# Moving the scatter of an expert pair between the two contraction halves of the next pair's gate and up products

## The chip, the cores and the metric

The kernel runs on one core of a Trainium2 chip. The metric is the device time of one execution in microseconds; the median of three runs stands for the kernel. It is written against the engines directly: each engine has its own program, and they meet only at semaphores.

## The reference, cut to what matters

The kernel computes one inference step of a two-layer backbone over 128 context and 128 latent tokens with 1024 channels. Each layer has two token mixers (attention and gated linear attention) and then a mixture of experts with 16 experts of width 512, of which two are chosen for each token inside its best group. All is float32. The change touches only the mixture of experts:

```
gates = jnp.sum(jax.nn.one_hot(top_idx, N_EXPERTS, dtype=jnp.float32) * top_w[..., None], axis=1)
act = jax.nn.silu(jnp.einsum('nd,edf->nef', hf, w_gate)) * jnp.einsum('nd,edf->nef', hf, w_up)
y = jnp.einsum('nef,efd->nd', act * gates[..., None].astype(act.dtype), w_down)
x = x + g2 * y
```

## The kernel before, in words

The dense part of a layer comes first, then the experts, in pairs: 8 pairs a layer, each with two experts of 64 token slots (with these inputs one pass is enough, since the trace shows 16 pairs in both layers). `expert_pair` on TensorE (L1000 to L1069) does for a pair q:

- the gate and up products (L1023) of the gathered rows `hg`, over 1024 channels in two contraction halves, kh 0 and kh 1, each in two parts and for two halves of the expert's columns. Half 0 of the columns is complete three quarters of the way through kh 1, half 1 at its end;
- `turn(0)` (L1044): the transposes of the activated half 0 of the columns, `aa`, into a PSUM bank. It waits for VectorE's activation (`m_act`) of that half;
- `scatter(q - 1)` (L971 to L983, products at L981), not in the first pair: the previous pair's output rows `yy`, 64 slots of each expert, times the turned gates `gwt`, which spreads them to their tokens. Eight products into the PSUM banks 4, 5, 7 and again 4; the last group waits until VectorE has added the first (`m_x`);
- `turn(1)` for half 1 of the columns;
- the down products (L1035) in two halves. Each waits for ScalarE's copy of its turned columns (`m_at_copied`) and for its weights. The first pair has `sort_rows` (L996) between them;
- `turn_gates(q)` (L968), the transposes of the gates that the next scatter needs.

After the last pair of a pass `scatter` is called once more, by itself (L1078).

ScalarE (`expert_pair`, L1342 to L1370) does for a pair, in this order: two sigmoids of the gate columns (L1347); the copy of turn 0 (recorded at the helper line L1092); then, behind it in its program, the `windows` for the next pair, for which it loads six registers from `starts` (L1306) and makes four copies of sorted rows into `hg`; the copy of turn 1; two copies of the down products into `yy`; the copy of the turned gates.

```
for half in range(2):
    act.wait_ge(m_at[l], q * 2 + 2 + half)
...
    copy(at_[:, 2 * half:2 * half + 2, :],
...
    elif half == 0:
        windows(q + 1, window_starts(pr + 1))
```

VectorE does `activate(q)` (L1856 and L1858, for each half of the columns one product with the gate and one with the up columns), `add_experts(q - 1)` (L1867: 16 instructions that add the scattered rows, scaled, to x) and `onehots` (L1843) for the next pair.

SyncE (SP) loads the weights. The pairs have 6 units of 2 MiB: units 0 and 1 are the gate and up weights of kh 0 for the two experts, 2 and 3 those of kh 1, 4 and 5 the two halves of the down weights. Each is loaded in two parts of 1 MiB (L441) into a ring of six slots, so a part can be loaded only when the previous pair has used that part of its unit; `expert_use` gives the semaphore for it. SP waits for one part after the other, in the order in which PE uses them. Units 0, 1 and 2 of pair 4 have a place of their own (`MORE`) and are loaded ahead of pair 0's products. Behind the last pair the next layer's dense units use the same ring.

Of the kernel before, what the change touches and what calls it, by code (L numbers as in the profile page):

```python
# [212 lines left out]
def build(nc, xT, consts, params, lparams, w_ada, w_in, w_pa, w_pb, w_out, w_gu, w_down,  # L213
# [4 lines left out]
    with ctx:  # L218
# [189 lines left out]
        def gu_unit(l, kh, e, in_more):  # L408
            return expert_space(l, 2 * kh + e, in_more).rearrange("p (c j k n) -> p c j k n", c=2, j=2, k=KH // 2)

        def down_unit(l, half):
            return expert_space(l, 4 + half, False).rearrange("p (e k n) -> p e k n", e=2, k=FT // 2)
# [114 lines left out]
        def _(pe):  # L527
# [120 lines left out]
            for l in range(LAYERS):  # L648
# [313 lines left out]
                def turn_gates(q):  # L962

                    pe.wait_ge(m_onehot[l], q + 2)
                    pe.wait_ge(m_x[l], q * 4 + X_DONE)
                    pe.wait_ge(m_gwt_copied[l], q + 1)
                    for s in range(S):
                        mm = pe.transpose(ps[:, 7, s * P:(s + 1) * P], gw[:, s, :], ident)  # L968
                    mm.then_inc(m_gwt[l], 1)

                def scatter(q):  # L971

                    pe.wait_ge(m_gwt_copied[l], q + 2)
                    for f in range(4):
                        if f % 2 == 0:
                            pe.wait_ge(m_y[l], q * 2 + 2 + f // 2)
                        if f in (0, 3):
                            pe.wait_ge(m_x[l], q * 4 + (1 if f else 0) + X_DONE)
                        for j in range(2):
                            k = 2 * f + j  # L980
                            mm = pe.matmul(ps[:, (4, 5, 7, 4)[f], j * NT:(j + 1) * NT], yy[:, k * P:(k + 1) * P], gwt,  # L981
                                           start=True, stop=True)
                        mm.then_inc(m_scat[l], 1)  # L983
# [16 lines left out]
                def expert_pair(pss, pr, in_more=False, later=False, first=False):  # L1000
                    q = pss * PAIRS + pr

                    pe.wait_ge(m_act[l], q * 2 + 1)
                    for kh in range(2):
                        for e in range(2):
                            u = 2 * kh + e
                            if u not in MORE:
                                pe.wait_ge(moe_full[l][u], q * 32 + 32)
                            elif in_more:
                                pe.wait_ge(more_full[l][u], pss * 32 + 32)  # L1010
                            else:

                                loads = pr if later else pr + 1
                                pe.wait_ge(moe_full[l][u], pss * (32 * (PAIRS - 1)) + loads * 32)
                        if kh == 0:
                            pe.wait_ge(m_hg[l], q * 4 + 5)
                        for part in range(2):
                            for half in range(2):
                                for kk in range(KH // 2):
                                    k = kh * KH + part * (KH // 2) + kk  # L1020
                                    for e in range(2):
                                        r = e * SLOTS
                                        mm = pe.matmul(ps[r:r + SLOTS, half, :].rearrange("p (j n) -> p j n", j=2),  # L1023
                                                       hg[:, k, e, 0:SLOTS],
                                                       gu_unit(l, kh, e, in_more)[:, part, :, kk, half * 256:(half + 1) * 256],
                                                       start=k == 0, stop=k == KT - 1)
                                if kh and part:
                                    mm.then_inc(m_gu[l][half], 1)
                            if not (kh and part):
                                mm.then_inc(m_rows[l], 1)  # L1030

                    def down(k, n):
                        for e in range(2):
                            r = e * SLOTS
                            mm = pe.matmul(ps[r:r + SLOTS, 2 + n, :], at_[:, k, r:r + SLOTS],  # L1035
                                           down_unit(l, k // 2)[:, e, k % 2, n * 512:(n + 1) * 512],
                                           start=k == 0, stop=k == FT - 1)
                        return mm

                    def turn(half):  # L1040
                        pe.wait_ge(m_act[l], q * 2 + 2 + half)
                        pe.wait_ge(m_at_copied[l], q * 2 + 1 + half)
                        for j in range(2):
                            mm = pe.transpose(ps[:, 6, (2 * half + j) * P:(2 * half + j + 1) * P],  # L1044
                                              aa[:, half, j * P:(j + 1) * P], ident)
                        mm.then_inc(m_at[l], 1)

                    turn(0)
                    if not first:
                        scatter(q - 1)  # L1050
                    turn(1)
                    pe.wait_ge(m_y[l], q * 2 + 1)
                    for half in range(2):
                        pe.wait_ge(m_at_copied[l], q * 2 + 2 + half)
                        pe.wait_ge(moe_full[l][4 + half], q * 32 + 32)
                        if half == 0:
                            for k in range(2):
                                for n in range(2):
                                    mm = down(k, n)
                            mm.then_inc(m_dn[l][0], 1)  # L1060
                            if first:
                                sort_rows(pss)
                        else:
                            for n in range(2):
                                down(2, n)
                                down(3, n).then_inc((m_dy[l], m_dn[l][1])[n], 1)
                    if first:
                        pe.wait_ge(m_rowcopied[l], pss * (2 * ROWS // P) + 2 * ROWS // P)
                    turn_gates(q)  # L1069
# [310 lines left out]
        def _(dve):  # L1380
# [132 lines left out]
            for l in range(LAYERS):  # L1513
# [336 lines left out]
                def activate(q):  # L1850

                    for half in range(2):
                        dve.wait_ge(m_sig[l], q * 2 + 2 + half)
                        dve.wait_ge(m_at[l], q * 2 + 1)
                        gate, up, e = ps[:, half, 0:256], ps[:, half, 256:512], eg[:, half, :]
                        dve.tensor_tensor(e, e, gate, ALU.mult).then_inc(m_silu[l], 1)  # L1856
                        dve.wait_ge(m_silu[l], q * 2 + 1 + half)
                        dve.tensor_tensor(aa[:, half, :], e, up, ALU.mult).then_inc(m_act[l], 1)  # L1858

                def add_experts(q):  # L1860

                    for f in range(4):
                        dve.wait_ge(m_scat[l], q * 4 + f + 2)
                        for j in range(2):
                            for s in range(S):
                                k, c = 2 * f + j, slice(s * T, (s + 1) * T)
                                ins = dve.scalar_tensor_tensor(  # L1867
                                    x[:, k, c], ps[:, (4, 5, 7, 4)[f], j * NT + s * T:j * NT + (s + 1) * T],
                                    mod[:, l, 40 + k, s:s + 1], x[:, k, c], ALU.mult, ALU.add)
                        ins.then_inc(m_x[l], 1)  # L1870
# [21 lines left out]
                with dve.Fori(0, passes) as pss:  # L1892
                    first = pss * PAIRS
                    activate(first)
                    onehots(1, first + 1)
                    with dve.Fori(1, PAIRS - 1) as pr:
                        q = pss * PAIRS + pr
                        activate(q)
                        add_experts(q - 1)
                        onehots(pr + 1, q + 1)  # L1900
                    last = pss * PAIRS + (PAIRS - 1)
                    next_windows(pss)
                    activate(last)
                    add_experts(last - 1)
                    onehots(0, last + 1)
                    add_experts(last)
                dve.wait_ge(m_x[l], passes * (4 * PAIRS) + X_DONE)
# [200 lines left out]
```

## Time and profile before

| | us |
|---|---|
| median of 3 runs (lowest, highest) | 1016.75 (1015.66, 1017.27) |
| the profiled execution: its time | 1016.9 |
| the profiled execution: its span | 1015.1 |
| PE busy in the span | 965.7 |
| VectorE busy | 383.4 |
| ScalarE busy | 237.9 |
| share of the hardware DMA queue in 16 engines' span | 75.1% |

All rows come from the one profiled execution, and times in them are counted from the start of its span; what lies around the span is 1.8 us. The experts of layer 0 stand at about 296 to 518 us, those of layer 1 at about 789 to 1012 us. PE is the product engine, PEld its weight loads, DVE is VectorE, ACT is ScalarE, SP is SyncE. A wait is named with its releaser: what ended it. "Issue" is time in which an engine waited for nothing that the profile shows. L1092 is the line of a helper that makes all of ScalarE's copies; its tiles tell which copy it is (`tmq` holds `hg`, `yy`, `at_` and `gwt`; a copy from `cst` is a window copy).

### The profile page before, as it was taken

How to read it: one execution, taken by the hardware profiler on the slowest of the kernel's cores; microseconds unless marked ns; L12 is line 12 of the kernel's file. 1: busy time of each engine (PE TensorE's matmuls, PEld its weight loads, DVE VectorE, ACT ScalarE, POOL GpSimd, SP SyncE). 2: the span in 40 equal slices, each digit the busy share in tenths (PEclk: the TensorE clock that was granted, in tenths of full speed). 3: DMA queues.
4: the chain of work that ended last, by engine and by line, in shares of the span. 5: the costliest groups of instructions: out<-in, count | busy, mean ns of one | idle time of the engine just before them, and what ended most of it. 6: DMA issues, size and time to landing. Idle time of an engine off the chain costs nothing.

```text
span 1015.1 us, 13671 instructions
## 1 busy us (share of the span) xinstructions
PE 965.7 (95%) x4910; PEld 566.2 (56%) x4910; DVE 383.4 (38%) x1011; ACT 237.9 (23%) x521; POOL 99.9 (10%) x85
## 2 busy tenths in 40 slices
PE   9999999989989999999899999999899899999997
PEld 3458876767845443443344688777686444344333
DVE  4098513782261222222351421248635222222134
ACT  2213223520023222221140312343201222222121
POOL 0000004631100000000000000066310000000000
PEclk9999999999999999999999999999999999999999
DMA  9999462156999999999997524240877999989993
GB/s 391 383 397 410 181 247 97 72 235 243 403 367 407 410 422 363 424 421 423 426 425 323 223 94 157 83 167 1 343 287 285 401 402 423 423 363 422 421 422 124
DMA packets 37378, 317.48 MB, mean 313 GB/s; under 512 B 4280, under 2 KB 4432, under 8 KB 5328
## 3 DMA queue, kind: packets, MB, share of 16 engines
q1 hardware_dynamic: 36144, 311.28, 75.1%
q0 software_dynamic: 1184, 5.53, 1.3%
q8 instruction: 32, 0.52, 0.2%
q14 instruction: 18, 0.15, 0.0%
HBM read 314.93 MB, written 1.86 MB: 312 GB/s over the span
## 4 chain that ended last, share of the span: by engine, by line
PE 77%; DMA 13%; DVE 4%; ACT 3%; issue 1%; SPq 0%; ACTq 0%; DVEq 0%
PE ps L1023 18%; DMA ring<-w_gu 12%; PE ps L563 11%; PE ps L1035 7%; PE ps L717 7%; PE ps L912 5%; PE ps L981 3%; PE ps L898 3%; PE ps L735 3%; PE ps L830 2%; PE ps L576 2%; PE ps L996 1%; DMA ring<-w_ada 1%; PE ps L673 1%; PE ps L543 1%
## 5 line engine op out<-in xcount | busy, mean ns | idle before, releaser
L1023 PE MATMUL ps<-ring,tmq 128*64 128x512 f32 x928 | 214.1, 602 | 17.2 <-DMA ring<-w_gu 13.7
L1023 PEld LDWEIGHTS ps<-ring,tmq 128*64 128x64 f32 x928 | 68.2, 138 | 143.6 <-issue 126.1
L563 PE MATMUL ps<-more,ring 128*128 128x256 f32 x512 | 114.3, 381 | 0.5 <-ACT more L1092 0.5
L1035 PE MATMUL ps<-ring,tmq 128*64 128x512 f32 x512 | 113.8, 596 | 0.0
L563 PEld LDWEIGHTS ps<-more,ring 128*128 128x128 f32 x512 | 96.1, 190 | 15.5 <-issue 2.5
L1856 DVE TENSOR_TENSOR tmq<-tmq,ps 128x256 f32<-128x256 f32 x32 | 13.5, 422 | 206.5 <-ACT tmq L1347 206.5
L1092 ACT ACTIVATE tmq<-ps 128x256 f32<-128x256 f32 (+3 forms) x124 | 55.6, 462 | 149.0 <-PE ps L717 62.8
L1035 PEld LDWEIGHTS ps<-ring,tmq 128*64 128x64 f32 x512 | 35.2, 137 | 65.7 <-issue 62.1
L717 PE MATMUL ps<-ring,more 128*128 128x512 f32 (+1 forms) x192 | 69.9, 523 | 0.0
L1867 DVE SCALAR_TENSOR_TENSOR x<-ps,mod,x 128x128 f32<-128x128 f32 x256 | 67.6, 342 | 1.9 <-PE ps L981 1.9
L1347 ACT ACTIVATE tmq<-ps 128x256 f32<-128x256 f32 x32 | 12.3, 384 | 226.6 <-PE ps L1023 226.6
L1843 DVE TENSOR_SCALAR tmq<-cst,st 128x64 f32<-128x64 f32 x72 | 17.8, 310 | 117.9 <-PE ps L968 117.2
L981 PE MATMUL ps<-tmq 128*128 128x256 f32 x256 | 58.6, 382 | 1.6 <-ACT tmq L1092 1.6
L912 PE MATMUL ps<-more,ring 128*128 128x256 f32 x256 | 56.4, 380 | 0.0
L717 PEld LDWEIGHTS ps<-ring,more 128*128 128x128 f32 x192 | 36.2, 190 | 32.9 <-issue 31.1
L912 PEld LDWEIGHTS ps<-more,ring 128*128 128x128 f32 x256 | 48.2, 190 | 7.1 <-issue 0.8
L981 PEld LDWEIGHTS ps<-tmq 128*128 128x128 f32 x256 | 47.3, 190 | 8.0 <-issue 2.0
L1092 ACT ACTIVATE tmq<-cst 128x512 f32 (+1 forms) x64 | 35.3, 622 | 47.9 <-issue 47.6
L1942 POOL TENSOR_TENSOR more<-tmq,cst 128x896 f32<-128x896 f32 x16 | 33.3, 2084 | 119.1 <-PE ps L766 109.4
L1479 DVE SCALAR_TENSOR_TENSOR wide<-ring,mixer 128x1024 f32<-128x1024 f32 x32 | 39.2, 1224 | 10.6 <-DMA mixer<-cs_dram 9.6
L543 PE MATMUL ps<-ring,cs 128*32 128x512 f32 x320 | 39.7, 611 | 1.0 <-DMA ring<-w_ada 1.0
L1956 POOL TENSOR_TENSOR mixer<-tmq,more 128x896 f32<-128x896 f32 x16 | 35.2, 2200 | 49.5 <-ACT more L1240 31.2
(256 smaller groups left out, 1036.0 us busy)
## 6 DMA issues: line engine op xcount, KB each, us to landing
ring<-w_gu SPq DMA_DIRECT2D x116, 1024.0 KB, 14.3
ring<-w_down SPq DMA_DIRECT2D x64, 1024.0 KB, 12.4
ring<-w_ada SPq DMA_DIRECT2D x24, 2048.0 KB, 10.9
ring<-w_in SPq DMA_DIRECT2D x14, 2048.0 KB, 17.1
ring<-w_out SPq DMA_DIRECT2D x4, 2048.0 KB, 11.1
more<-w_gu SPq DMA_DIRECT2D x8, 1024.0 KB, 14.1
cst<-consts SPq DMA_DIRECT2D x2, 2080.0 KB, 15.8
ring<-w_in SPq DMA_DIRECT2D x4, 1024.0 KB, 24.1
```

The source lines that it names most:

```text
L543: mm = pe.matmul(ps[j:j + 32, 7, :], cs[:, k, :], w[:, k, :], start=k < 4, stop=k >= 4)
L563: mm = pe.matmul(ps[:, 5, i * NT:(i + 1) * NT], w[:, k, m * P:(m + 1) * P], h[:, k, :], start=k == 0, stop=k == KT - 1)
L717: mm = pe.matmul(ps[:, n % 4, 0:cols], h[:, k, (n % 2) * T:(n % 2) * T + T], w[:, k, 0:cols], start=i == 0, stop=i == KT - 1)
L912: mm = pe.matmul(ps[:, 4 + b % 4, (b // 4) * NT:(b // 4 + 1) * NT], w[:, k, (b % 4) * P:(b % 4 + 1) * P], sga[:, k, :], start=k == 0, stop ...
L981: mm = pe.matmul(ps[:, (4, 5, 7, 4)[f], j * NT:(j + 1) * NT], yy[:, k * P:(k + 1) * P], gwt, start=True, stop=True)
L1023: mm = pe.matmul(ps[r:r + SLOTS, half, :].rearrange("p (j n) -> p j n", j=2), hg[:, k, e, 0:SLOTS], gu_unit(l, kh, e, in_more)[:, part, :, ...
L1035: mm = pe.matmul(ps[r:r + SLOTS, 2 + n, :], at_[:, k, r:r + SLOTS], down_unit(l, k // 2)[:, e, k % 2, n * 512:(n + 1) * 512], start=k == 0 ...
L1092: return act.activation(out, in_, ACT.Copy, scale=scale)
L1479: link(dve.scalar_tensor_tensor(wide[:, :], w[:, i, :], 1.0, cs_rows[:, s, :], ALU.mult, ALU.mult, accum_out=mod[:, l, 4 * a + i, s:s + 1]))
L1867: ins = dve.scalar_tensor_tensor(x[:, k, c], ps[:, (4, 5, 7, 4)[f], j * NT + s * T:j * NT + (s + 1) * T], mod[:, l, 40 + k, s:s + 1], x[:, ...
L1942: pool.tensor_tensor(qz, q, C("side").rearrange("p (v t) -> p v t", t=T), ALU.mult).then_inc(g_qz, 1)
L1956: pool.tensor_tensor(halves(ke), kh.unsqueeze(1).to_broadcast([P, LEVELS, 2, HALF]), level_view(e), ALU.mult).then_inc(g_ke, 1)
```

## The change

In TensorE's program the scatter of the previous pair is called between kh 0 and kh 1 of the gate and up products, no longer between the two turns. In VectorE's program the adds of the previous pair, which read what the scatter wrote, come ahead of the activation, in the loop and for the last pair. The first pair of a pass, ScalarE's program and SP's program are as before.

```
--- before.py
+++ after.py
@@ -1028,6 +1028,8 @@
                                     mm.then_inc(m_gu[l][half], 1)
                             if not (kh and part):
                                 mm.then_inc(m_rows[l], 1)
+                        if kh == 0 and not first:
+                            scatter(q - 1)
 
                     def down(k, n):
                         for e in range(2):
@@ -1046,8 +1048,6 @@
                         mm.then_inc(m_at[l], 1)
 
                     turn(0)
-                    if not first:
-                        scatter(q - 1)
                     turn(1)
                     pe.wait_ge(m_y[l], q * 2 + 1)
                     for half in range(2):
@@ -1895,13 +1895,13 @@
                     onehots(1, first + 1)
                     with dve.Fori(1, PAIRS - 1) as pr:
                         q = pss * PAIRS + pr
+                        add_experts(q - 1)
                         activate(q)
-                        add_experts(q - 1)
                         onehots(pr + 1, q + 1)
                     last = pss * PAIRS + (PAIRS - 1)
                     next_windows(pss)
+                    add_experts(last - 1)
                     activate(last)
-                    add_experts(last - 1)
                     onehots(0, last + 1)
                     add_experts(last)
                 dve.wait_ge(m_x[l], passes * (4 * PAIRS) + X_DONE)
```

## Rows read from the trace of the kernel before

**Rows 1.** The page, busy time of an engine and the DMA share by slices
```profile
PE 965.7 (95%) x4910; PEld 566.2 (56%) x4910; DVE 383.4 (38%) x1011; ACT 237.9 (23%) x521; POOL 99.9 (10%) x85
...
DMA  9999462156999999999997524240877999989993
```

**Rows 2.** The chain that ended last, shares of the span by engine
```profile
PE 77%; DMA 13%; DVE 4%; ACT 3%; issue 1%; SPq 0%; ACTq 0%; DVEq 0%
```

**Rows 3.** The list of waits: who waited for whom, total us, times, longest
```profile
PE ps L1023 <- DMA ring<-w_gu: 13.7, 7, 2.7
```

**Rows 4.** Windows: stretch, its us, busy PE, PEld, DVE, ACT, POOL, clock, DMA, GB/s
```profile
326.38:351.74 25.36, 25.36 (x120) 10.39 (x119) 6.87 (x24) 5.11 (x12) 0.00 (x0) 1.00 0.98 398
...
377.08:404.06 26.98, 25.57 (x119) 10.26 (x118) 6.87 (x24) 5.10 (x12) 0.00 (x0) 1.00 0.91 368
...
404.00:454.00 50.00, 50.00 (x236) 20.57 (x234) 13.72 (x48) 9.99 (x22) 0.00 (x0) 1.00 1.01 422
...
326.38:513.70 187.32, 179.86 (x827) 72.80 (x826) 49.46 (x176) 35.64 (x78) 0.00 (x0) 0.99 1.00 412
819.42:1005.44 186.02, 179.80 (x827) 72.67 (x826) 49.36 (x176) 35.63 (x78) 0.00 (x0) 0.99 0.94 387
```

**Rows 5.** Timeline of PE, pairs 6 and 7: start, us, work, idle time before it
```profile
463.70 7.09 PE L1023 MATMUL ps<-ring,tmq 128*64 128x512 f32 x32 [1.86 <-DMA ring<-w_gu]
...
483.76 7.09 PE L1023 MATMUL ps<-ring,tmq 128*64 128x512 f32 x32 [1.51 <-DMA ring<-w_gu]
...
493.53 8.78 PE L1023 MATMUL ps<-ring,tmq 128*64 128x512 f32 x32 [2.68 <-DMA ring<-w_gu]
```

**Rows 6.** Timeline of pair 1 around its turns
```profile
340.27 0.44 PE L1044 MATMUL ps<-cst,tmq 128*128 128x128 f32 x2
...
340.54 3.66 PE L981 MATMUL ps<-tmq 128*128 128x256 f32 x16
...
340.82 0.38 ACT L1092 ACTIVATE tmq<-ps 128x256 f32<-128x256 f32 x1
...
341.65 4.23 DVE L1867 SCALAR_TENSOR_TENSOR x<-ps,mod,x 128x128 f32<-128x128 f32 x16
344.04 0.38 PE L1044 MATMUL ps<-cst,tmq 128*128 128x128 f32 x2
344.35 7.09 PE L1035 MATMUL ps<-ring,tmq 128*64 128x512 f32 x32
344.67 2.22 ACT L1092 ACTIVATE tmq<-cst 128x512 f32 x4 [3.46 <-issue]
346.79 0.36 ACT L1092 ACTIVATE tmq<-ps 128x256 f32<-128x256 f32 x1
```

**Rows 7.** One line, L1306: count, duration in ns min/median/max, first and last start
```profile
L1306 ACTq TENSOR_LOAD <-starts x96: 271/278/297, 310.4 to 997.3; - x96
```

**Rows 8.** Timeline of pair 0, which has no scatter, around its turns
```profile
309.68 0.44 PE L1044 MATMUL ps<-cst,tmq 128*128 128x128 f32 x2
...
311.13 0.44 PE L1044 MATMUL ps<-cst,tmq 128*128 128x128 f32 x2 [1.02 <-DVE tmq L1858]
...
311.50 3.65 PE L1035 MATMUL ps<-ring,tmq 128*64 128x512 f32 x16
```

**Rows 9.** The chain in order of time at the kernel's end: start, us, what
```profile
1005.68 0.39 ACT tmq L1092
1006.06 0.23 issue
1006.29 1.14 PE ps L981 x4
```

**Rows 10.** The line of the weight loads, L441: from issue to landing
```profile
DMA to landing us min/median/max: 4.9/14.1/22.7
```

**Rows 11.** Windows after waits of PE in layer 1, columns as in group 4
```profile
985.00:990.00 5.00, 3.05 (x14) 1.06 (x16) 0.00 (x0) 0.00 (x0) 0.00 (x0) 1.00 1.01 421
...
957.20:966.00 8.80, 8.80 (x33) 2.68 (x34) 0.84 (x2) 0.40 (x2) 0.00 (x0) 0.81 1.02 425
```

More of the change, by code:

```diff
@@ L1030, in expert_pair @@
                                 mm.then_inc(m_rows[l], 1)
+                        if kh == 0 and not first:
+                            scatter(q - 1)
                     def down(k, n):
@@ L1048, in expert_pair @@
                     turn(0)
-                    if not first:
-                        scatter(q - 1)
                     turn(1)
@@ L1897, in _ @@
                         q = pss * PAIRS + pr
+                        add_experts(q - 1)
                         activate(q)
-                        add_experts(q - 1)
                         onehots(pr + 1, q + 1)
@@ L1902, in _ @@
                     next_windows(pss)
+                    add_experts(last - 1)
                     activate(last)
-                    add_experts(last - 1)
                     onehots(0, last + 1)
```

## The prediction

> **What bounds the kernel now.** I read the page first. TensorE (PE) is busy 95% of the span, and the DMA row of the slices stands at 9, once at 8, in both expert stretches (about the 12th to 20th and the 32nd to 39th slice) [rows 1]. So the product engine and the weight stream both run nearly full there, and the change touches only those stretches. The chain that ended last is PE for 77% and DMA for 13% [rows 2], and the list of waits gives the DMA part a place: the gate and up products waited for w_gu units, 7 times, 13.7 us in all [rows 3]. The windows by expert pair then say which of the two leads when. A pair that waits for nothing takes PE 25.36 us [rows 4]. A pair needs 12 parts of 1 MiB; at the 422 GB/s of the undisturbed stretch that is 2.48 us a part, 29.8 us a pair [rows 4]. So PE is the quicker by 4.4 us, starts with a stock of loaded units, and eats it up: the waits of the timeline come in pairs 6 and 7 (1.86, 1.51 and 2.68 us) [rows 5], and in pair 3 the same. From the start of pair 1's products to the end of pair 7 a layer takes 187.32 and 186.02 us, where seven pairs without a wait would take 177.5 [rows 4]. So 9.8 and 8.5 us a layer are waits for weights, with some slower products after them.
>
> The last view is the timeline around the two turns (the transposes of the activated halves) in pair 1: what stands in the place from which the scatter is taken. Turn 0 starts at 340.27 (I call this moment t), the scatter runs 340.54 to 344.04, turn 1 follows, and the down products start at 344.35, t + 4.08 [rows 6]. Under that scatter ScalarE (ACT) and VectorE (DVE) finish the second half's activation, and ACT then does more: the copy of turn 0 at 340.82, a gap of 3.46 us put down to "issue", four window copies (2.22 us), and only then the copy of turn 1, at 346.79 to 347.15, t + 6.88 [rows 6]. The gap is no idle time: it holds the six register loads of the window starts (96 TENSOR_LOADs in 16 pairs) and the arithmetic on them [rows 7]. The second half of the down products waits for that last copy. Today it comes at t + 4.08 + 3.51 = t + 7.59, half of the 7.09 us row and then some, so the copy is ready about 0.7 us early [rows 6]. **That small margin exists only because of the scatter.**
>
> **The change, part by part.** The scatter itself is moved, not changed: 8 products, 16 PE instructions, 3.50 us from its first product to turn 1 [rows 6]. It issues no DMA; its waits (the turned gates, the two halves of the y rows) are signalled while kh 0's first products still run. PE pays 3.50 us there and is spared 3.50 here, net 0. Borders of its new place aren't in the trace: I bound them by -0.1 us (the weights of neighbours overlap as well as here) and +0.3 us a pair (turn 1 costs 0.31 us with its borders, 344.04 to 344.35 [rows 6]); I take 0, since the scatter's own rows show no gap at either border.
>
> Turn 1 without cover. The trace of before already has one pair in the new order: pair 0, which has no scatter. There turn 0 starts at 309.68, turn 1 at 311.13 after a wait of 1.02 us for DVE, the down products at 311.50, which is t + 1.82 [rows 8]. The scatter's removal gives back 4.08 - 1.82 = 2.26 us, not 3.50. Cost: 3.50 - 2.26 = +1.24 us a pair.
>
> The copy of turn 1. Nothing on ACT moves: its order is still copy, loads, windows, copy, counted from turn 0, so it ends at t + 6.88 as now. The first half of the down products now ends at t + 1.82 + 3.51 = t + 5.33. A product waiting for ACT starts 0.23 us after the copy's end, by the one hand-over that the chain shows [rows 9]. So the second half starts at t + 7.11, a **new wait of 1.78 us** a pair (1.5 if the hand-over is free). Behind it stand, on PE, the second down half, the gate turns and the next pair's products, so nothing covers it.
>
> DVE. The adds of the previous pair (4.23 us [rows 6]) move ahead of the activation. They start about 1 us into the scatter and end some 2 us after it, while the first half's gate and up products need 5.2 us after the scatter, half of kh 1 and half of the rest (5.2 = three quarters of 7.0). So the activation isn't delayed; the cover is those products. Cost 0. The scatter's last product group waits for the first adds, which come as early as before. Cost 0.
>
> The sum on PE. A pair takes 25.36 + 1.24 + 1.78 = 28.38 us. Seven pairs take 198.7 us from the same starts: layer 0 ends its pairs at 326.38 + 198.7 = 525.1 instead of 513.70, +11.4; layer 1 at 819.42 + 198.7 = 1018.1 instead of 1005.44, +12.7. Pair 0 is as before, and so is everything after the pairs.
>
> Do waits for weights still add to that? SP is moved past nothing, but its buffers come free later: the kh 1 units by 3.50 us, the last down unit 0.8 us earlier in the pair. What matters is whether the stream, now slower than PE by only 1.5 us a pair, still runs PE down. The stream ran dry once a layer, before pair 4, whose first three units were loaded ahead (368 GB/s in that pair) [rows 4]. By my times it is dry last when pair 3's first down half is done: pair 3 starts at 383.1, its turn 0 comes 13.89 + 3.50 = 17.4 us later, and its first down half ends 5.33 us after that, at 405.8. The fastest landing took 4.9 us against 2.48 of transfer [rows 10], so the stream restarts at about 408 and then moves 40 parts without a break (4 for pair 4, 12 each for pairs 5 to 7). Those that close a need are the 20th, the 32nd and the 36th: pair 6's first units have landed by 408 + 20 x 2.48 + 2 = 460 against a need at 468.3; pair 7's at 489 against 496.7; pair 7's kh 1 units at 499 against 507.1. So PE is never starved; it has 7 us to spare at the tightest place, and the expert stretch turns from stream-bound to PE-bound. The stream ends about 6 us later than now, PE about 11, so the next layer's first units are no closer to being late.
>
> Total: 11.4 + 12.7 = 24.1 us; the profiled execution took 1016.9 us (span 1015.1), 0.15 above the median of 1016.75, so **1016.9 + 24.1 = 1041.0 us**. Own range of this case: 14 pairs by -0.35 us (border -0.1, hand-over free) to +0.3 us give 1036 to 1045.
>
> **The rivals.** 1. *The clock.* The new order puts two waits, 1.02 and 1.78 us, into 7 us of each pair. After the waits of 1.51 and 2.68 us in pair 7 its kh 1 products took 8.78 instead of 7.0 us [rows 5], and the stretch 957.2 to 966 after a wait had a granted clock of 0.81 [rows 11], a mix of the 1.2 and 2.4 GHz levels. If each pair fell so once, 14 x 1.78 = 25 us more, 1066; if half of them did, 1053. Against it: 985 to 990 has PE idle for 1.95 us and kept 1.00 [rows 11], and pair 6 waited 1.86 us before kh 1 and still took 7.0 us for it (463.70 to 470.7) [rows 5], so a wait as long as the longer new one needn't cost it. Chance 0.12. The Trainium skill (TensorE: Matmul & The Clock Gate, section HAM oscillation — how this bites in real kernels) describes loops in which waits between groups of products throttle the array anew in every iteration. [...]
>
> 2. *The margin isn't lost.* If the copy of turn 1 came earlier (its loads running ahead of turn 0), the second wait is gone and a pair takes 26.6 us. Seven take 186.2: 512.6 and 1005.6, so layer 0 gains 1.1 and layer 1 nothing. If turn 1 too were covered the stream would be the bound and the scatter would have left the tail behind the last landing: 493.53 + 7.0 + 1.82 + 7.02 + 0.35 = 509.7, 4.0 us early, and 2.3 in layer 1. So 1010.6 to 1015.5, **faster or the same**; it decides at a pair of 26.6 us, the least that the stream and the ends of before leave room for. Against it: the loads start only after the copy of turn 0 at every turn of rows 6 and 7, and ACT's program has them behind it. Chance 0.08, of it 0.05 faster by over 0.2%.
>
> 3. *In part.* The loads take less time where they don't run beside the scatter, and the wait is 0.5 to 1.2 us: 18 to 8 us less than the forecast, 1023 to 1033. Chance 0.06.
>
> **How the numbers follow.** The forecast has 0.74, and its time is the predicted one. The range takes its own range, the milder half of rival 1 and the upper part of rival 3: 1030 to 1053; left out are rival 2, the worst of rival 1 and half of rival 3. A measurement of this kernel can tell about 0.2% (2 us) from no change. Faster 0.05; same 0.03; slower 0.74 + 0.12 + 0.06 = 0.92.
>
> **What would show it.** Right: pair windows of 28.4 us at clock 1.00; PE L1023 no longer waiting for DMA; a new wait of PE L1035 for ACT's copy, 1.8 us in 14 pairs, and of turn 1 for DVE, 1.0 us; the slices' DMA rate lower in the expert stretches. The second half starting before t + 6.9, or pairs of 26.5 us, would make rival 2 right; a granted clock below 0.95 over the expert pairs, rival 1; waits for w_gu that stay would mean that I have the stream's slack wrong.

## The result and the profile after

The changed kernel takes 1043.76 us (median of 4 runs, 1042.61 to 1047.02), the kernel before 1017.01 us beside it: a ratio of 1.0248, with a 95% interval of 1.0218 to 1.0278. It is slower by 2.5%. The forecast was 1041.0 us in a range of 1030 to 1053. The profiled execution took 1043.26 us (span 1041.4), 26.4 us more than that of before.

The page of the changed kernel, first its busy times, DMA slices and chain, then two of the costliest groups:

```profile
PE 971.4 (93%) x4910; PEld 562.7 (54%) x4910; DVE 383.7 (37%) x1011; ACT 237.8 (23%) x521; POOL 99.9 (10%) x85
...
DMA  9999454076999997999995442242687999799991
...
PE 81%; ACT 5%; DVE 4%; ACTq 4%; issue 4%; DMA 1%; SPq 0%; DVEq 0%
...
L1023 PE MATMUL ps<-ring,tmq 128*64 128x512 f32 x928 | 212.2, 595 | 3.5 <-issue 3.5
L1037 PE MATMUL ps<-ring,tmq 128*64 128x512 f32 x512 | 116.9, 598 | 19.1 <-ACT tmq L1092 19.1
```

PE's busy time has hardly grown (971.4 against 965.7 us); the rest is idle. The DMA part of the chain has gone from 13% to 1%, and ACT with its queue, 3% before, is at 9% [rows 2]. The gate and up products wait for no weights any more [rows 3]; in their place the down products (L1037 is L1035 of before) wait 19.1 us for a copy of ScalarE. The list of waits of the changed kernel puts that beside the second new wait (us in total, times, longest):

```profile
PE ps L1037 <- ACT tmq L1092: 19.1, 14, 1.4
PE ps L1046 <- DVE tmq L1858: 16.4, 16, 1.0
```

The first has 14 instances, one in each pair that has a scatter. The second is turn 1 waiting for VectorE's activation: 16 times now, where only the two first pairs had it before.

The windows of single pairs and of both layers' seven pairs (columns as in group 4 of the rows):

```profile
325.66:354.23 28.57, 26.10 (x120) 10.11 (x119) 6.89 (x24) 5.10 (x12) 0.00 (x0) 1.00 0.99 400
...
382.77:411.32 28.55, 26.10 (x119) 10.10 (x119) 6.90 (x24) 5.10 (x12) 0.00 (x0) 1.00 0.73 277
325.66:525.07 199.41, 182.70 (x827) 70.73 (x826) 49.67 (x176) 35.66 (x78) 0.00 (x0) 1.00 0.97 398
832.33:1031.78 199.45, 182.69 (x827) 70.72 (x826) 49.55 (x176) 35.61 (x78) 0.00 (x0) 1.00 0.88 361
```

Pair 1 takes 28.57 us where it took 25.36 [rows 4], and every later pair takes the same: the seven last 199.41 us, 7 x 28.5. In pair 3 the weight stream now runs at 277 GB/s (368 before) and PE still waits for no weights: there the stream waits for PE to free its buffers. The two layers' pairs cost 199.41 - 187.32 = 12.1 and 199.45 - 186.02 = 13.4 us more, 25.5 of the 26.3 us of span.

Pair 1 of the changed kernel in the timeline:

```profile
325.66 7.09 PE L1023 MATMUL ps<-ring,tmq 128*64 128x512 f32 x32
...
332.68 3.72 PE L981 MATMUL ps<-tmq 128*128 128x256 f32 x16
333.85 4.23 DVE L1867 SCALAR_TENSOR_TENSOR x<-ps,mod,x 128x128 f32<-128x128 f32 x16 [7.10 <-PE ps L981]
336.33 7.09 PE L1023 MATMUL ps<-ring,tmq 128*64 128x512 f32 x32
341.84 0.38 ACT L1347 ACTIVATE tmq<-ps 128x256 f32<-128x256 f32 x1 [15.56 <-PE ps L1023]
...
343.35 0.44 PE L1046 MATMUL ps<-cst,tmq 128*128 128x128 f32 x2
...
343.90 0.38 ACT L1092 ACTIVATE tmq<-ps 128x256 f32<-128x256 f32 x1
...
344.81 0.44 PE L1046 MATMUL ps<-cst,tmq 128*128 128x128 f32 x2 [1.02 <-DVE tmq L1858]
345.18 3.65 PE L1037 MATMUL ps<-ring,tmq 128*64 128x512 f32 x16
347.75 2.21 ACT L1092 ACTIVATE tmq<-cst 128x512 f32 x4 [3.46 <-issue]
...
349.86 0.36 ACT L1092 ACTIVATE tmq<-ps 128x256 f32<-128x256 f32 x1
350.28 3.65 PE L1037 MATMUL ps<-ring,tmq 128*64 128x512 f32 x16 [1.45 <-ACT tmq L1092]
```

Read it from turn 0 at 343.35. Turn 1 comes 1.46 us later after a wait of 1.02, as in the pair without a scatter [rows 8]. ACT does what it did, at the same distances [rows 6]: copy, 3.46 us of register loads, window copies, and the copy of turn 1, which ends at 350.22, t + 6.87. The first down half is long done; the second starts 0.06 us after that copy. The adds end at 338.08, well before the sigmoid of half 0 at 341.84.

### The profile page after: what moved, and what is told of

Same layout as the page of the kernel before. It is cut to its first block, busy times and chain, and to the rows that moved or that the text cites. A ratio compares the mean times of both kernels' runs of the same rounds, so it can differ in the third digit from the quotient of the medians.

```text
span 1041.4 us, 13671 instructions
## 1 busy us (share of the span) xinstructions
PE 971.4 (93%) x4910; PEld 562.7 (54%) x4910; DVE 383.7 (37%) x1011; ACT 237.8 (23%) x521; POOL 99.9 (10%) x85
## 4 chain that ended last, share of the span: by engine, by line
PE 81%; ACT 5%; DVE 4%; ACTq 4%; issue 4%; DMA 1%; SPq 0%; DVEq 0%
PE ps L1023 22%; PE ps L563 11%; PE ps L717 7%; PE ps L1037 6%; PE ps L981 5%; PE ps L912 5%; ACTq L1306 4%; PE ps L898 3%; PE ps L735 3%; PE ps L830 2%; ACT tmq L1092 2%; PE ps L576 2%; DMA ring<-w_ada 1%; PE ps L996 1%; PE ps L673 1%
## 5 line engine op out<-in xcount | busy, mean ns | idle before, releaser
L1037 PE MATMUL ps<-ring,tmq 128*64 128x512 f32 x512 | 116.9, 598 | 19.1 <-ACT tmq L1092 19.1
L1023 PEld LDWEIGHTS ps<-ring,tmq 128*64 128x64 f32 x928 | 66.6, 137 | 122.6 <-issue 122.6
L1037 PEld LDWEIGHTS ps<-ring,tmq 128*64 128x64 f32 x512 | 33.9, 136 | 89.2 <-issue 57.5
L981 PEld LDWEIGHTS ps<-tmq 128*128 128x128 f32 x256 | 47.3, 190 | 19.2 <-issue 13.4
```

## The experiments

Where nothing else is said, an experiment starts from the changed kernel. Ratios are to the kernel before, run on the same chip.

**The copy of turn 1 first.** ScalarE copies turn 1 before it loads the window starts and copies the windows.

```
-                        if half == 0 and last:
+                        if half == 1 and last:
...
-                        elif half == 0:
+                        elif half == 1 and not first:
                             windows(q + 1, window_starts(pr + 1))
```

> The changed kernel, with ScalarE's copy of turn 1 put ahead of the register loads and window copies. Theory (the exposed copy and the exposed activation are the cost, PE is the bound): the wait of the second down half for the copy (1.44 us a pair) goes, the 1.0 us wait of turn 1 stays, a pair takes 27.1 us, 14 pairs give back up to 20 us; some waits for weights return at the end of each layer: 1023 to 1027 us. Rival (buffers that come free later starve the stream): the copy's wait goes but waits for w_gu take its place, 1040 us or more. Rival (the clock): nothing in the clock rows changes, it can't explain a difference.

Measured: 1020.6 us (ratio 1.0028, 1.001 to 1.0046). The timeline of pair 1 in this kernel:

```profile
342.45 0.44 PE L1046 MATMUL ps<-cst,tmq 128*128 128x128 f32 x2
...
343.92 0.44 PE L1046 MATMUL ps<-cst,tmq 128*128 128x128 f32 x2 [1.03 <-DVE tmq L1858]
344.29 7.09 PE L1037 MATMUL ps<-ring,tmq 128*64 128x512 f32 x32
344.39 0.38 ACT L1092 ACTIVATE tmq<-ps 128x256 f32<-128x256 f32 x1 [1.00 <-PE ps L1046]
...
348.27 2.22 ACT L1092 ACTIVATE tmq<-cst 128x512 f32 x4 [3.50 <-issue]
```

The down products run through as one piece of 7.09 us; ACT's loads and window copies lie beside them, and turn 1 still waits 1.03. The pair takes 351.67 - 324.77 = 26.90 us, 1.67 less than before this edit. So the place of one copy of 0.36 us in ScalarE's program carries most of the loss: 14 x 1.67 = 23 of the 26 us. The time lies 2.4 us below the expected interval, because the pair is 0.2 us shorter than I wrote and the waits for weights that I expected to return didn't: at pairs of 26.9 us the stream still keeps ahead in all seven.

**The register loads early.** The six loads stand ahead of the sigmoids in pairs 1 to 6; the window copies stay where they are.

```
+                    if not first and not last:
+                        ahead = window_starts(pr + 1)
                     for half in range(2):
                         act.wait_ge(m_gu[l][half], q + 2)
...
-                            windows(q + 1, window_starts(pr + 1))
+                            windows(q + 1, ahead)
```

> The changed kernel, with the six register loads moved ahead of the sigmoids for pairs 1 to 6 (the window copies stay ahead of the copy of turn 1). If it is the loads that hold the copy back, the copy comes at t + 3.7 instead of t + 6.9 in those 12 pairs and the wait goes as in the run before: 1024 to 1029 us. If it is the window copies, at most 0.3 us a pair is won: about 1040 us.

Measured: 1023.95 us (1.0055, 1.0039 to 1.0071). Pair 1, from turn 0 on:

```profile
344.10 0.44 PE L1046 MATMUL ps<-cst,tmq 128*128 128x128 f32 x2
...
344.65 0.38 ACT L1092 ACTIVATE tmq<-ps 128x256 f32<-128x256 f32 x1
344.93 2.20 ACT L1092 ACTIVATE tmq<-cst 128x512 f32 x4
...
345.93 7.09 PE L1037 MATMUL ps<-ring,tmq 128*64 128x512 f32 x32
...
347.03 0.37 ACT L1092 ACTIVATE tmq<-ps 128x256 f32<-128x256 f32 x1
```

The gap before the window copies is gone, the copy of turn 1 ends at 347.40, t + 3.3 (t + 3.7 was expected), and the down products run through. Only the two last pairs, where the loads stayed between the two copies, still wait (2 times, 2.0 us in all). So the "issue" gap is the loads, and moving them alone brings the copy in time. That doesn't clear the window copies: they take 2.2 us, more than the 1.59 us by which the second down half is late, so by the trace moving them alone should be enough too. That version wasn't built.

**The adds split.** Only the first group's adds stand ahead of the activation, the other twelve behind it.

```
-                        add_experts(q - 1)
+                        add_experts(q - 1, range(1))
                         activate(q)
+                        add_experts(q - 1, range(1, 4))
```

> The changed kernel, with only the first group's adds (which the last scatter group needs) ahead of the activation and the other twelve behind it. Theory: VectorE's order costs nothing, since all adds end before the first half's gate and up products: 1043 us, pairs of 28.57 us. Rival (the adds ahead of the activation delay it): a pair gets shorter, 14 times its share, below 1040 us.

Measured: 1044.15 us (1.0254, 1.0223 to 1.0285). Its pair 1 takes 353.32 - 324.75 = 28.57 us, to the hundredth that of the changed kernel. VectorE's new order costs nothing. A version with no adds ahead of the activation wasn't built. By the program it could not run: the last scatter group in its new place waits for the first adds, and the activation waits for kh 1 behind that group, so the two engines would wait for each other.

**Lighter weights, before and after.** Half of each part of the down weights isn't loaded, in the kernel before and in the changed one.

```
+                    c = slice(part * UNIT // 2, part * UNIT // 2 + UNIT // 4)
                     src = w_down[l, bass.ds(pr, 1), u - 4, :, c]
```

> The kernel before, loading only half of each part of the down weights (the products read what stands in the rest of the buffer). It takes 1/6 of the stream away. Theory: the kernel before was held back by the stream by 9.8 and 8.5 us in its two layers, so it falls to seven pairs of 25.35 us: 998 to 1001 us. If the stream cost nothing, 1016 us.

> The changed kernel with the same half of the down weights left out. Theory: PE alone sets the pair of 28.57 us, so nothing changes: 1043 us (1041 to 1044), and the difference to the kernel before, with the same left out, is 14 x 3.2 = 45 us. Rival (later buffers starve the stream): lighter weights give time back, 1030 us or less.

Measured: 1000.59 us (0.9828, 0.9796 to 0.9859) and 1043.59 us (1.0248, 1.0217 to 1.028). Neither kernel computes the full result, but both run the 4910 TensorE instructions of the full kernels. The kernel before loses all its waits for weights and 17 us; the changed one gains nothing. Between the two lie 43.9 us in the profiled executions (1042.71 - 998.81), close to 14 times the growth of a pair: 12 x 3.22 us, and 2.8 us for each of the two last pairs, where the copy is 0.4 us less late: 44 us. **So the change costs PE 44 us of its own time, and 18 of these the kernel before had been spending in waits for weights.** Late buffers have no part in it.

**Half of the scatter moved.** Two of its four groups stand between the contraction halves, two between the turns.

```
-                            scatter(q - 1)
+                            scatter(q - 1, range(2))
...
                     turn(0)
+                    if not first:
+                        scatter(q - 1, range(2, 4))
                     turn(1)
```

> The changed kernel with half of the scatter (two groups of four) between the contraction halves and half between the turns, the adds split the same way. Theory: two groups, 1.75 us, cover the 1.0 us of turn 1, and 1.0 us of wait for the copy is left: a pair of 26.8 us, 1018 to 1022 us. If only the whole scatter covers turn 1, about 1032 us.

Measured: 1020.08 us (1.0024, 1.0007 to 1.0041). The timeline of its pair 1:

```profile
342.12 0.44 PE L1046 MATMUL ps<-cst,tmq 128*128 128x128 f32 x2
...
342.40 1.89 PE L981 MATMUL ps<-tmq 128*128 128x256 f32 x8
...
344.13 0.38 PE L1046 MATMUL ps<-cst,tmq 128*128 128x128 f32 x2
344.44 3.65 PE L1037 MATMUL ps<-ring,tmq 128*64 128x512 f32 x16
...
348.64 0.36 ACT L1094 ACTIVATE tmq<-ps 128x256 f32<-128x256 f32 x1
349.06 3.65 PE L1037 MATMUL ps<-ring,tmq 128*64 128x512 f32 x16 [0.96 <-ACT tmq L1094]
```

Turn 1 has no wait: two groups cover the activation. The copy is still late, by 0.96 us. The pair takes 353.01 - 326.16 = 26.85 us.

**Control: ScalarE's order in the kernel before.** The edit of the first experiment, in the kernel before.

> Control: the kernel before with the same ScalarE order (copy of turn 1 ahead of the loads and the window copies). Theory: there the copy was 0.7 us early anyway, so nothing changes: 1016 to 1018 us. If the order of ScalarE's work is worth something by itself, it shows here.

Measured: 1018.39 us (1.0006, 0.9989 to 1.0023). The order is worth nothing where the scatter gives the copy its time.

**Both covers, in every pair.** Half of the scatter moved, and the copy of turn 1 first.

> The split of the scatter in every pair (two groups of four between the contraction halves, two between the turns) together with ScalarE's copy of turn 1 ahead of its loads and window copies. Theory: both waits are gone, a pair without a wait for weights takes 25.6 us (25.35 and the borders of the moved half), which the stream's 29.8 us can't follow, so waits for weights return as in the kernel before, and the end of a layer comes half a scatter (1.75 us) sooner: 1011 to 1016 us. If the moved half delays the stream as much as it shortens the end, 1016 to 1018 us.

Measured: 1010.93 us (0.9945, 0.9925 to 0.9965), **0.5% faster than the kernel before**, by an interval that leaves out 1. PE in its pair 7 of layer 0:

```profile
483.21 7.09 PE L1023 MATMUL ps<-ring,tmq 128*64 128x512 f32 x32 [2.68 <-DMA ring<-w_gu]
490.23 1.99 PE L981 MATMUL ps<-tmq 128*128 128x256 f32 x8
492.96 7.09 PE L1023 MATMUL ps<-ring,tmq 128*64 128x512 f32 x32 [0.74 <-DMA ring<-w_gu]
499.98 0.44 PE L1046 MATMUL ps<-cst,tmq 128*128 128x128 f32 x2
500.26 1.89 PE L981 MATMUL ps<-tmq 128*128 128x256 f32 x8
501.99 0.38 PE L1046 MATMUL ps<-cst,tmq 128*128 128x128 f32 x2
502.30 7.09 PE L1037 MATMUL ps<-ring,tmq 128*64 128x512 f32 x32
```

The wait for the kh 1 weights is now partly filled by the moved half: 0.74 us where the kernel before waited 2.68 [rows 5]. Behind the last weights half a scatter less is left to do. That the kh 1 products take 7.09 us here and not 8.78 isn't shown to be the move's doing: in layer 1 of the same execution the kh 0 products of pair 7 took 8.56 us after a wait of 2.66, and the granted clock of the whole execution was 0.993 against 0.994 in the kernel before.

**In the last pair only.** The same from the kernel before, with the split of scatter and adds in pair 7 alone; then with three groups moved instead of two; then with two groups and ScalarE's order as before.

```
+                        if kh == 0 and last:
+                            scatter(q - 1, range(2))
...
-                        scatter(q - 1)
+                        scatter(q - 1, range(2 if last else 0, 4))
```

> From the kernel before: the scatter is split (two groups between the contraction halves, two between the turns) in the last pair of a pass only, with the adds of that pair split the same way, and ScalarE copies turn 1 first. In that pair PE waits 2.5 to 2.7 us for the kh 1 weights. Theory: half the scatter goes into that wait, 1.75 us a layer, and the shorter wait may keep the clock up in layer 0 (1.7 us): 1011 to 1014 us. If the wait for the weights grows by what is put ahead of it, or the tail is set by something else, 1016 us or more.

> As the last-pair kernel, with three groups of the scatter between the contraction halves and one between the turns. There PE still waited 0.74 and 0.62 us for the kh 1 weights, and the third group takes 0.87 us; one group (0.87 us) covers nearly all of turn 1's 1.0 us. Theory: 0.5 us a layer better than the last-pair kernel, about 1 us, too little to tell in the times: 1011 to 1013 us; the timeline shows the wait for the weights gone. If turn 1 isn't covered by one group, 0 gain.

> As the last-pair kernel, with ScalarE's order as in the kernel before. The copy of turn 1 then comes at t + 6.5 against a second down half that could start at t + 5.9 in the last pair. Theory: a wait of about 0.9 us in the last pair of each layer returns, 1.8 us in all: 1013 to 1015 us. If the gain of the last-pair kernel came from ScalarE's order, 1017 us.

Measured: 1012.51 us (0.9948, 0.9929 to 0.9966), 1011.17 us (0.9942, 0.9925 to 0.9959) and 1012.21 us (0.996, 0.9944 to 0.9975). With three groups the kh 1 products of layer 0's pair 7 follow the scatter without a wait (494.35) and turn 1 waits 0.16 us. With ScalarE's order as before the second down half waits 0.52 us for the copy there, not the 0.9 that I expected. The times of these three and of the version with both covers in every pair can't be told apart.

Where the gain lies can be read behind the last weights. PE in pair 7 of layer 1, first in the kernel before, then in the last-pair kernel (two groups):

```profile
986.95 7.09 PE L1023 MATMUL ps<-ring,tmq 128*64 128x512 f32 x32 [2.53 <-DMA ring<-w_gu]
...
1006.29 3.72 PE L981 MATMUL ps<-tmq 128*128 128x256 f32 x16 [0.79 <-ACT tmq L1092]
```

```profile
982.26 7.09 PE L1023 MATMUL ps<-ring,tmq 128*64 128x512 f32 x32 [0.62 <-DMA ring<-w_gu]
...
999.66 3.72 PE L981 MATMUL ps<-tmq 128*128 128x256 f32 x16 [0.60 <-ACT tmq L1095]
```

From the kh 1 products to the scatter that ends the layer it is 19.34 us before and 17.40 after: 1.94 us less, of which 1.75 are the moved half. In two layers that is 3.9 us of the 4.6 between the medians (1017.12 and 1012.51); the rest is within the interval. So the gain lies where the last weights arrive; it needs the move in one pair, and only half of it.

## Why the prediction was right

**The bound.** Right. The kernel before was held back by the stream (17 us came back with lighter weights, against the 9.8 + 8.5 of the prediction), and the changed one by PE alone. The hand count of the stream found that it would have 7 us to spare; no wait for w_gu is left, and none came back even at pairs of 26.9 us.

**The exposed activation.** +1.24 us a pair was read from pair 0. Measured: from turn 0 to the down products 1.83 us (343.35 to 345.18), as in pair 0 (1.82), so +1.25.

**The copy of turn 1.** The largest term, and it held: start of the second down half at t + 6.93 instead of the t + 7.11 that I had. The hand-over took 0.06 us (350.22 to 350.28), not the 0.23 of the one I took it from [rows 9]. The late start is 1.59 us a pair (350.28 against 348.69), 0.19 below the 1.78. The first two experiments show that it is this copy, and that it is late by what ScalarE does ahead of it: without the loads there it comes in time. The split adds show that it isn't VectorE.

**The scatter's borders.** Taken as 0 with bounds of -0.1 and +0.3; this is the term that was mis-sized. From the start of the pair to turn 0 it is 17.69 us (325.66 to 343.35), where 13.89 + 3.50 = 17.39 was expected: **+0.30 us a pair**, the upper bound. The scatter and its borders take 3.65 us here (332.68 to 336.33) and 3.50 between the turns, and kh 0 and kh 1 apart take 7.02 each where together they took 13.89. Part of the cost of a run of products is paid anew when it is cut in two.

**The adds.** Cost 0, as predicted (the split adds).

**The sum.** 28.38 us a pair were predicted and 28.57 measured: +0.30 for the borders, -0.18 for the hand-over and +0.07 behind it, where the down products run in two pieces. That two terms were off in opposite directions is luck, and it makes the pair look better forecast than its parts. Over 14 pairs it is 25.5 us instead of 24.1. The rest of the 26.3 us of span isn't from the change's place: the first experts start 0.7 us earlier, the dense part of layer 1 takes 1.5 us more (the last section), and the end is the same. Two numbers of the working are wrong and carry nothing: by its own times the last down unit comes free 3.0 us later in the pair, not 0.8 us earlier, and rival 2's upper end is 1016.9 - 1.1 = 1015.8 us, not 1015.5.

**The rivals.** The clock stayed at 1.00 in all 14 pairs, the new waits of 1.02 and 1.45 us notwithstanding; the loop that the Trainium skill (TensorE: Matmul & The Clock Gate, section HAM oscillation — how this bites in real kernels) describes waits about 3 to 5 us in each iteration, longer than either of them, so it doesn't speak for a fall here, and none came. Rival 2, a copy that isn't late, was built with the early loads. The pair was then 26.9 us and not the 26.6 from which it decides, by the borders, and the kernel stayed slower than before (1.0055). Rival 3 fell: the loads take the same 3.46 us beside other work.

## What to carry to other kernels

Before a filler is moved, list everything that another engine finishes under it, not only what its neighbour waits for: here the scatter covered 1.0 us of waiting for an activation and, one step later, a copy that stood behind 3.46 us of register loads and 2.2 us of window copies, with 0.7 us in hand. An engine's idle gap named "issue" can be such a row of loads, and then it sets when the work behind it is done. If a filler is wanted in two places, move the part that the old place can spare, first where the engine already waits: half the scatter in the last pair alone gave 0.5%, the whole scatter in every pair cost 2.5%.

## What the runs showed of the hardware

The granted clock fell in one execution and not in another at the same instructions. PE of the changed kernel in the dense part of layer 1, where the window 731.35 to 751.35 has a granted clock of 0.91:

```profile
738.27 0.66 PE L880 MATMUL ps<-cst,tmq 128*128 128x128 f32 x4 [1.82 <-DVE tmq L1654]
738.86 0.39 PE L883 MATMUL ps<-cst,mod 128*16 128x128 f32 x2
739.70 15.62 PE L898 MATMUL ps<-more,ring 128*128 128x256 f32 x64 [0.46 <-ACT lrt L1092]
```

The kernel before ran the same instructions after the same waits (1.82 and 0.46 us) in 14.05 us, with a clock of 1.00. The same happened after waits for weights. In the last-pair kernel PE waited 2.56 us before kh 1 of pair 6 in layer 0 and 2.35 us in layer 1:

```profile
462.68 7.09 PE L1023 MATMUL ps<-ring,tmq 128*64 128x512 f32 x32 [2.56 <-DMA ring<-w_gu]
...
952.45 8.78 PE L1023 MATMUL ps<-ring,tmq 128*64 128x512 f32 x32 [2.35 <-DMA ring<-w_gu]
```

The longer wait cost nothing and the shorter one 1.7 us. In a kernel of 1000 us one such fall is 0.15%, which is part of why differences below 0.2% aren't told here.
